# Two hybrid layer stacks on one core: the factors of the row norms move to the copies out of PSUM, sections beside inner norms are multiplied by token block, and the layers are written out over one running weight ring

## The reference

```
for layer in 0, 1:                       # block one
    h = rms_norm(x, norm_w)              # x * rsqrt(mean(x*x) + 1e-6) * w, row by row
    qa ka va za qb kb vb zb ga gb = split(h @ w_in)          # 1024 x 10240
    ya = dilated_mixture(rope(qa), rope(ka), va) * silu(za)  # 16 heads
    yb = rms_norm(diff_attention(rope(qb), rope(kb), vb), subln_w) * silu(zb)
    x = x + (sigmoid(ga) * (ya @ w_proj_a) + sigmoid(gb) * (yb @ w_proj_b)) @ w_out
x = rms_norm(x, final_norm_w)
for layer in 0, 1:                       # block two
    h = rms_norm(x, pre_mix_g)
    dq dk dv dz db da sq sk sv ga gb = split(h @ w_in_2)
    y_a = gated_delta_rule(conv_silu(dq, dk, dv), db, da) -> head norm, gate dz -> @ w_up_dn
    y_b = sliding_window_attention(rope(sq), rope(sk), sv, sinks) @ w_up_sw
    x = x + rms_norm((sigmoid(ga) * y_a + sigmoid(gb) * y_b) @ w_o, post_mix_g)
    h2 = rms_norm(x, pre_mlp_g)
    x = x + rms_norm(relu(h2 @ w_ff1)**2 @ w_ff2, post_mlp_g)
```

## Time and profile before

| | |
|---|---|
| median of 3 runs | 2010.72 us (2007.05 to 2010.78) |
| the profiled execution | 2010.85 us, of which the span in the trace is 2009.1 us |
| mean granted TensorE clock | 0.973 |
| TensorE matmuls | 1877.0 us busy, 93% of the span |
| VectorE, ScalarE, GpSimd | 1199.0, 908.9 and 211.1 us |

### The profile page before, as it was taken

One profiled execution on the slowest core, in us unless ns is written; L12 is line 12 of the kernel. 1 busy time (PEld: TensorE's weight loads), 2 busy tenths in 40 slices (PEclk: granted clock), 3 DMA queues, 4 the chain that ended last, 5 costly groups with the idle time before them and its releaser, 6 DMA issues.

```text
span 2009.1 us, 28952 instructions
## 1 busy us (share of the span) xinstructions
PE 1877.0 (93%) x9719; PEld 1545.9 (77%) x9719; DVE 1199.0 (60%) x2321; ACT 908.9 (45%) x1600; POOL 211.1 (11%) x237
## 2 busy tenths in 40 slices
PE   5999989899998997999999979997999999979997
PEld 4877768787786786777888868886777888868886
DVE  4656657565655665676656655554587655655554
ACT  4344455444435544464343444444465333444443
POOL 0302000020110000202222000000201322100000
PEclk9999999999999998998999989998999999999999
DMA  6543534455343445332212435552622222354552
GB/s 227 173 146 115 167 105 169 148 172 166 123 147 111 141 153 173 128 104 84 85 64 85 147 126 190 188 170 86 209 92 96 67 84 66 124 167 147 182 186 73
DMA packets 136900, 270.50 MB, mean 135 GB/s; under 512 B 5556, under 2 KB 8360, under 8 KB 136744
## 3 DMA queue, kind: packets, MB, share of 16 engines
q1 hardware_dynamic: 134868, 265.74, 40.3%
q10 hardware_dynamic: 1876, 2.78, 0.4%
HBM read 267.45 MB, written 1.05 MB: 134 GB/s over the span
## 4 chain that ended last, share of the span: by engine, by line
PE 52%; issue 36%; DVE 7%; ACT 3%; POOL 2%; DVEq 0%; ACTq 0%; POOLq 0%
PE bank L349 11%; PE bank L351 11%; PE bank L350 11%; PE bank L1400 3%; PE bank L372 2%; PE bank L1414 2%; PE bank L1413 1%; DVE buf L1666 1%; PE bank L1319 1%; ACT scratch L575 1%; DVE scratch L777 1%; PE bank L466 1%; PE bank L458 1%; PE bank L456 1%; DVE lo L332 1%
## 5 line engine op out<-in xcount | busy, mean ns | idle before, releaser
L349 PE MATMUL bank<-hi,xh 128*128 128x512 f32 (+1 forms) x2016 | 820.9, 407 | 6.1 <-DVE xl L1637 3.3
L351 PE MATMUL bank<-hi,xl 128*128 128x512 f32 (+1 forms) x2016 | 791.0, 392 | 0.0
L350 PE MATMUL bank<-lo,xh 128*128 128x512 f32 (+1 forms) x2016 | 789.3, 391 | 0.0
L325 ACT ACTIVATE hi<-raw 128x1024 fp32r<-128x1024 f32 (+1 forms) x512 | 528.8, 1036 | 352.0 <-PE bank L351 349.7
L332 DVE TENSOR_TENSOR lo<-raw,hi 128x1024 fp32r<-128x1024 f32 (+1 forms) x512 | 612.9, 1212 | 97.1 <-ACT hi L325 96.5
L351 PEld LDWEIGHTS bank<-hi,xl 128*128 128x128 f32 x2016 | 382.4, 190 | 82.6
L349 PEld LDWEIGHTS bank<-hi,xh 128*128 128x128 f32 x2016 | 383.6, 190 | 78.9 <-issue 8.8
L350 PEld LDWEIGHTS bank<-lo,xh 128*128 128x128 f32 x2016 | 384.2, 191 | 69.1
L372 PE MATMUL bank<-square,buf 128*128 128x128 f32 x584 | 88.0, 273 | 19.2 <-ACT scratch L585 11.6
L372 PEld LDWEIGHTS bank<-square,buf 128*128 128x128 f32 x584 | 70.1, 140 | 36.1 <-ACT scratch L585 12.6
L1593 ACT ACTIVATE scratch<-bank 128x512 f32<-128x512 f32 x48 | 28.7, 598 | 145.3 <-PE bank L1400 145.3
(11 more groups left out here) (262 smaller groups left out, 1972.9 us busy)
## 6 DMA issues: line engine op xcount, KB each, us to landing
raw<-in_w_in SPq DMA_DIRECT2D x136, 1024.0 KB, 5.1
raw<-in_w_ff SPq DMA_DIRECT2D x64, 1024.0 KB, 5.2
raw<-in_w_proj_a SPq DMA_DIRECT2D x8, 1024.0 KB, 5.2
raw<-in_w_proj_b SPq DMA_DIRECT2D x8, 1024.0 KB, 5.1
raw<-in_w_out SPq DMA_DIRECT2D x8, 1024.0 KB, 5.1
raw<-in_w_up_sw SPq DMA_DIRECT2D x8, 1024.0 KB, 5.1
raw<-in_w_up_dn SPq DMA_DIRECT2D x8, 1024.0 KB, 5.2
raw<-in_w_o SPq DMA_DIRECT2D x8, 1024.0 KB, 5.8
```

The costliest lines, as they stand in the source:

```text
L325: act.activation(self.hi[g % RING][:, 0:w], src, ACT.Copy).then_inc(self.hi_ready, 1)
L349: pe.matmul(out, xh[:, row, t], self.hi[slot][:, w], start=first, stop=False)
L350: pe.matmul(out, xh[:, row, t], self.lo[slot][:, w], start=False, stop=False)
L351: mm = pe.matmul(out, xl[:, row, t], self.hi[slot][:, w], start=False, stop=last)
```

## The change

1. **Row factors at the copies.** The norms of a section's input no longer stand ahead of its turns. x itself is turned (`turn_input`, plain transposes) and cut with the column gain; ScalarE's sums of squares (`stat`) and GpSimd's factor (`rms`) run beside the products, and the factor `r` (or half of it) is the scale of the copies out of PSUM: `tensor_copy` becomes `tensor_scalar`, tanh and relu get a scale by row, and where values were not scaled (`va`, `za`, `vb`, `zb`, `zz`) it goes into the heads' factors on GpSimd (`a_scaled`, `head_scaled`). For the final norm the gains are multiplied together (`first_gain`); VectorE still writes the normalized x (`x_final`), after the last turn, and the factor is formed in two steps. Products with `relu` squared use `mid_r` twice.
2. **Steps ahead of the boundary.** Steps marked `ahead` belong to the next layer but stand in the list of this one: `turn h 0` and `1` inside the last job of `out`.
3. **Token blocks one after the other** (`run_by_rows`): for `oo1`, `up0`, the two last `dn` jobs, and `sq0` of the second layer of block two, all 4 pieces are multiplied for block 0 (`first`), then all 4 for block 1 (`second`, which alone frees the ring's slots). The norm after the product and the next turns (`post_y`, `post_x`, `turn_rows`) are done for a token block at a time.
4. **Layers written out, one ring.** No `Fori`: both layers of both blocks are straight code over one numbering of pieces, and ScalarE, VectorE and SyncE run ahead over the ends of the layers.
5. **Order of small things.** `ba0` comes after `sq0` in 4 pieces instead of ahead of it in 8; the `ya` turns come ahead of the attention's part of their steps, and all in TURN; the turns of `f7` stand between the pieces of `dn6`.

```diff
+def ahead(steps):
+    return [("ahead", *what) for what in steps]
+def rows_turns(name, tb):
+    return [("turn_rows", name, tb, half) for half in range(2)]
 def plan_one(layer):
-    p.step("norm")
-    start_turns(p, "h", sec("qa", 0))
+    if layer == 0:
+        p.steps += [("turn", "h", 0), ("turn", "h", 1)]
+    p.run(sec("qa", 0), [[("turn", "h", 2), ("stat", 0)], [("turn", "h", 3), ("stat", 1), ("rstd",)]])
...
-    p.run(sec("gb", 9), [a + b for a, b in zip(work[4:12], [[], []] + turns("ya") + [[], []])])
+    p.run(sec("gb", 9), [b + a for a, b in zip(work[4:12], [[], []] + turns("ya") + [[], []])])
...
-    p.run(section("out", "w_out", 0, 1), turns("mix", 2))
+    p.run(section("out", "w_out", 0, 1), turns("mix", 2) + [[], []] + [ahead(t) for t in turns("h", 0, 2)]
+          + [ahead([("final_row",), ("stat", 0)]) if layer == DEPTH - 1 else []])
...
+    def run_by_rows(self, jobs, first, second):
+        start = len(self.pieces)
...
+        for kind, between in (("first", first), ("second", second)):
+            for g, steps in enumerate(between):
+                self.steps += [(kind, start + g, start)] + steps
 def plan_two(layer):
-    p.step("norm")
-    start_turns(p, "h", [Job("ba0", "w_in_2", 0, at_sw, KB, small, 2, 0, 0, (2, 3))])
-    p.run(sec("sq", at_sw + small), [[("decay",)], [], [("decay_sum",)]])
+    sq = sec("sq", at_sw + small)
+    if layer == 0:
+        p.run(sq[:1], [[("stat", 1), ("turn", "h", 2), ("rstd",)], [("turn", "h", 3), ("x_final",), ("stat_final",), ("rstd_final",)]])
+    else:
+        p.run_by_rows(sq[:1], [[], [], [], rows_turns("h", 1) + [("stat_rows", 1), ("rstd",)]], [[], [], [], [("evac", "sq0")]])
+    p.run([Job("ba0", "w_in_2", 0, at_sw, KB, small, 4, 0, 0, SCORE)])
+    p.run(sq[1:], [[("decay",)], [], [("decay_sum",)]])
...
-    p.run(section("oo", "w_o_2", 0, 1), turns("mix", 2))
-    p.step("post", 0)
-    p.step("norm_mlp")
+    y = lambda i, c, tb: [("post_y", i, c, tb)]
+    oo = section("oo", "w_o_2", 0, 1)
+    p.run(oo[:1], turns("mix", 2))
+    p.run_by_rows(oo[1:], [y(0, 0, 0) + y(0, 0, 1), [], [], y(0, 1, 0) + [("post_x", 0, 0)]],
+                  [[], [], [], rows_turns("h2", 0) + y(0, 1, 1) + [("post_x", 0, 1), ("mid_stat", 0)]])
...
+    p.run_by_rows(up_(0), [[], [], [], rows_turns("h2", 1) + [("mid_stat", 1), ("mid_r",)]], [[], [], [], [("evac", "up0")]])
+    for j in range(parts - 1):
+        p.run(up_(j + 1), f_turns(j))
+        if j < parts - 2:
+            p.run(dn(j))
+    p.run(dn(parts - 2), [[], [("turn", f"f{parts - 1}", 0)], [("turn", f"f{parts - 1}", 1)], []])
+    following = [ahead(rows_turns("h", 0)), ahead([("stat_rows", 0)])] if layer < DEPTH - 1 else [[], []]
+    p.run_by_rows(dn(parts - 1), [[], y(1, 0, 0), [], y(1, 1, 0) + [("post_x", 1, 0)]],
+                  [[], y(1, 0, 1), [], following[0] + y(1, 1, 1) + [("post_x", 1, 1)] + following[1]])
...
+def turn_input(pe, core, s, b, f):
+    core.free(pe, b)
+    for tb in range(TB):
+        x_rows_ready(pe, core, s, tb, f // 2)
+    turn_fill(None, pe, core, core.bank[b], core.x, f).then_inc(*s.up("turned", ("h", f)))
...
+def rms(pool, s, waits, means, out, key):
+    pool.wait_ge(*s.at("mean", waits[0]))
+    pool.tensor_scalar(out, means[0], 1e-6, None, ALU.add).then_inc(*s.up("rms_first", key))
...
+    pool.tensor_tensor(out, out, means[1], ALU.add).then_inc(*s.up("rms_sum", key))
...
+    pool.tensor_tensor(out, out, s.minus_half[:, 0:out.shape[-1]], ALU.pow).then_inc(*s.up("rms", key))
...
-                            ins = dve.tensor_copy(role[name][:, tb, cols], B[job.banks[tb]][:, :])
+                            ins = dve.tensor_scalar(role[name][:, tb, cols], B[job.banks[tb]][:, :],
+                                                    t.r[:, s.stage, tb:tb + 1], None, ALU.mult)
...
+                if kind in ("piece", "second"):
+                    core.split_lo(dve, base + arg + LO_LEAD + 1)
+                if kind == "first":
+                    core.split_lo(dve, base + min(arg + LO_LEAD + 1, what[2] + RING))
...
+                if kind == "post_y":
+                    c, tb = what[2:]
...
+                    dve.tensor_tensor(ys[:, tb, cols], B[2 * c + tb][:, :], kd_T[:, arg, cols], ALU.mult)\
+                       .then_inc(*up("post_y", (arg, c, tb)))
...
+                if kind == "turn_rows":
+                    tb, half = what[2:]
+                    for j in range(4):
+                        n = 4 * half + j
+                        dve.wait_ge(*at("high", (arg, tb, 4 * half + 3)))
+                        ins_ = dve.scalar_tensor_tensor(core.xl[0][:, n, tb * P:tb * P + P],
+                                                        B[(TURN, OUT)[half]][:, j * P:j * P + P], rows_gain(arg, n),
+                                                        core.xh[0][:, n, tb * P:tb * P + P].bitcast(F32), ALU.mult, ALU.subtract)
```

More of the change, by code:

```diff
@@ new lines, in split_lo, with multiply @@
+    def split_lo(self, dve, upto):
+        for g in range(self.lo_at, min(upto, len(self.pieces))):
+            src, w = self.piece_raw(g)
+            dve.wait_ge(self.hi_ready, g + 1)
+            dve.tensor_tensor(self.lo[g % RING][:, 0:w], src, self.hi[g % RING][:, 0:w].bitcast(F32),
+                              ALU.subtract).then_inc(self.lo_ready, 1)
+            self.lo_at = g + 1
+    def multiply(self, pe, g, rows=(0, 1), blocks=(0, 1)):
+        job, n = self.pieces[g]
+        pe.wait_ge(self.lo_ready, g + 1)
@@ L344, in multiply @@
             w = slice(kk * c, kk * c + c)
-            for tb in range(TB):
+            for tb in blocks:
                 out, t = self.bank[job.banks[tb]][:, 0:c], slice(tb * P, tb * P + P)
@@ L392, in block_one @@
     t = core.t1
-    P_ = len(plan.pieces)
-    base = 0
     at, up = s.at, s.up
@@ L403, in _ @@
     def _(pe):
-        with pe.Fori(0, DEPTH) as layer:
-            s.layer = layer
-            last_read = {}
-            def free(b):
-                if b in last_read:
-                    pe.wait_ge(*at(*last_read[b]))
+        for plan in plans:
+            layer, base = plan.layer, plan.base
             turn_at = 0
-            for what in plan.steps:
+            for what in plan.all_steps(s):
                 kind, arg = what[0], what[1] if len(what) > 1 else None
@@ L1978, in build @@
 def build(nc, ins, out, tally=None):
     with ExitStack() as ctx:
-        core = Core(nc, ctx)
-        names = ["setup", "one", "final", "setup2", "two"] + ["end"]
+        plans = [plan_one(layer) for layer in range(DEPTH)] + [plan_two(layer) for layer in range(DEPTH)]
+        for stage, plan in enumerate(plans):
+            plan.close(sum(len(done.pieces) for done in plans[:stage]), stage)
+        core = Core(nc, ctx, ins, plans)
+        names = ["setup", "main", "setup2", "end"]
         sig = {n: Signals(nc, ctx, n, tally and tally[n]) for n in names}
-        sig["two"].after = sig["one"]
```

834 lines of the change are left out of this document (460 added, 374 removed).

## The result

| | before | after |
|---|---|---|
| median of the runs | 2010.75 us (2007.05 to 2012.64) | 1938.78 us (1937.78 to 1940.03) |
| ratio | | 0.9643, 95% interval 0.9632 to 0.9655 |
| span of the profiled execution | 2009.1 us | 1937.3 us |
| mean granted clock | 0.973 | 0.987 |

The account below looks back on a forecast made before the run. TensorE, busy 93% of the span, bounds the kernel, so the gain is its removed stops less new ones. Terms sum to 80.3 us: 2010.85 - 80.3 = 1930.5, stated as 1930 us; 8-in-10 range 1917 to 1950.

Parts of the forecast that it names:

- The stops of the outer norms: TensorE's stops at layer and block boundaries and the end: gains of 9.5, 14.2, 10.5 and 4.9 us.
- the one wait that was named: Block one to two: VectorE's sq0 copy waits for the doubled norm, making ba0's third split late by 1.1 us (0 to 4).
- Inner norms: Norms around oo1 and up0, twice: 18.4 us falls to 9.3, a gain of 9.1 each, 18.2 us.
- the waits behind L1382: Transposes, copies and cuts directly ahead of the matmul at token-block switches: TensorE waits about 2.3 us, six times.
- the first rival: Clock falls at six token-block switches, 1.7 us each, up to 3.4: 1940 to 1950 us; chance 0.12.
- `ya`: Four turns' waits and low clock per layer, 10.2 us, leave two head-turn waits of 0.7: gain 17.6 us.
- the third rival: At ya, b_turn waits 2.9 us instead and the clock falls as before: 1945 us; chance 0.10.
- Costs put at nothing: the scale at the copies: Scaling copies out of PSUM adds 0.06 to 0.09 us each, hidden by the section's next pieces.
- The ring running dry: Second rival: slots freed only in second passes; five token-block jobs wait 5 us more each: 1955 us; chance 0.10.
- late code: Fourth rival: doubled program text loads late, TensorE waits per block: 2060 us at 1.5 us each; chance 0.02.

Follow-up runs that it names:

- the last two runs: Changed kernel with turns of sk and sq later, token-block transposes earlier, post_x behind up0's first piece: 1920.23 us; the same plus the ya turns' other banks: 1919.93 us.
- three edits: Changed kernel with turns of sk and sq one piece later, token-block transposes one piece earlier, post_x of block 1 behind up0's first piece: 1920.23 us, ratio 0.9550.

## Why the prediction was right, and where it was not

- **The stops of the outer norms** (9.5 + 14.2 + 10.5 + 4.9 predicted, 9.7 + 14.1 + 11.5 + 5.0 in the traces): right, place by place, with the one wait that was named, 0.73 us for 1.1.
- **Inner norms**: the mechanism and the waits behind L1382 were right (2.17 for 2.3). In layer 1 the clock fell at two of its switches (1743.8 and 1754.0), which is the first rival in part: 1.9 us, the gain at that place in four other traces where it stays up, out of a price of up to 10. How many of the six fall was luck: with waits of 2.00 us at each, none fell in the trace with the turns of q later, two in those with the waits filled and `ya` undone, four in that with the banks of `ya`, and all six in that without the scale. The run with the transposes earlier shows that most of the 2.17 us was no cost of the change as such.
- **`ya`**: the mechanism was right, the term mis-sized. It reckoned with copies that start at once; one of ScalarE's stands behind a split of 1.04 us and squares, so the head's turn waits 2.34 and not 0.7. That is the third rival's wait without its low clock. 15.7 and not 17.6; the run with this part alone gives 13, with the low clock that the third rival expected.
- **"Costs put at nothing: the scale at the copies".** This is the step that failed. It said that the section's next pieces hide the longer copies. At `sq1` they hid nothing, since there was a wait already, 1.78 us at L372 of the kernel before: the copies feed GpSimd's rotation, and TensorE's turn waits for that. 0.49 us of copies lengthened the wait (the run without the scale takes 0.41 and 0.53 back), 0.9 us in both layers. The whole place costs 4.7 us more than before, the greater part of the 8.7 by which the sum was off, and the larger share of that is the clock, 1.00 behind the wait before and 0.50 now. That share is not shown to come from the scale: without the scale the clock falls as well, and with `ya` undone it stays up in layer 0 behind the full 2.57 us. The prediction had no term for low clock at this place, and what decides it stays open. The run with the turns later takes all of the stop away.
- **What is left of the 7.4**, 2.7 us: 1.5 of it is a stretch of low clock of 10.2 us from 1460.5, where before there were 6.8 us from 1522.1; the rest is small steps. TensorE is busy in all of it, the first 7 us of it with the 32 matmuls of 128x1 of L1441 (L1319 before). All four stretches of low clock in the changed kernel that stand at no long wait (863.1, 910.9, 1460.5, 1511.7) lie in or right behind such a run of 32. No run here changes these matmuls, so that they are the cause isn't shown.
- **The ring running dry** (second rival) and **late code** (fourth): nothing of either in the trace. Pieces follow at 2.72 us in the long sections, and ScalarE waits for weights twice, 2.0 us in all, as before. The queue that loads program has 78 packets where it had 86: the fourth rival took it that straight code would be more to load.
- **The clock on the whole.** The stretches at 0.50 contain 69.8 us of TensorE's busy time in the kernel before and 46.5 in the changed one, 30.7 and 27.3 in the last two runs. Half of the first difference, some 11.6 us, is part of the 72. I had booked it in part at the places where it fell; the runs with the waits filled and with `ya` undone show that it can't be booked place by place.

The longer wait in `dk` has 0.8 - 0.4 = 0.4 us in layer 0 that no run settles; GpSimd's operations there took 0.2 us more in sum.

## What to carry to other kernels

When a cost is put at nothing because "the next piece hides it", follow the result to its last reader: here it went through VectorE and GpSimd to a TensorE turn that already waited, and a listed wait has no slack at all. Sort an engine's stops by what stands directly ahead of the late matmul in each queue; moving such work one piece earlier, or its reader one piece later, was worth 18.6 us here for three edits of a line or two. Waits of this kind add up when removed; low clock saved at one place need not stay saved.
